# Low parts of the weights by a negated high part and an accumulating DMA, mixer passes written out, values split once

## The chip, the cores and the metric

One NeuronCore of a Trainium2 chip runs the kernel. The metric is the device time of one execution in microseconds (us). Engines are called as the profile calls them: PE (TensorE, matmul), PEld (its weight loads), DVE (VectorE), ACT (ScalarE), POOL (GpSimd), SP (SyncE, which here only issues DMAs).

## The reference

One encoder block over 512 tokens of width 1024, in fp32:

```
mod = silu(c) @ w_ada + b_ada                 # six vectors of 1024
h   = rmsnorm(x) * (1 + sc1) + sh1
B, C, u, q, k, v, gA, gB = split(h @ w_in)    # 6656 columns; 16 query heads, 4 key/value heads of 64
yA  = B * dwconv3(C * u)
yB  = windowed attention(q, k, v)             # |t-s| <= 128, q and k normed, ALiBi, a sink per head
x   = x + g1 * ((sigmoid(gA)*yA + sigmoid(gB)*yB) @ w_o)
h   = rmsnorm(x) * (1 + sc2) + sh2
a, b = split(h @ w_up)                        # 2816 columns each
x   = x + g2 * ((gelu(dwconv3(a) + bias) * b) @ w_down)
```

## The kernel before, in words

**Three products for each.** Every large product is taken in split form. A fp32 matrix is cut into a high part in the format f32r and a low part, which is the matrix minus its high part; `three` (L652 to L654) adds high·high, low·high and high·low in PSUM. So all weights must be split on the chip, and the change is about who makes their low part.

**The weight pipeline.** Weights come in 64 loads numbered n. A load is 256 columns of one weight matrix for 8 blocks of 128 rows, 1 MB in rows of 1 KB (`load`, L274, issued by SP), into slot n % 2 of `w_raw`. It has two units u of 128 columns. For each unit ACT copies `w_raw` to `w_hi` (`high`, L415), and POOL subtracts, `w_lo = w_raw - w_hi` (`low`, L341). Each step waits for the one before: `high(n)` for the load and until PE has used both units of n - 2; `low(n)` for `high(n)`; PE for the low part of its unit; `load(n + 2)` for both low parts of n, since it overwrites `w_raw`. Load 0 is the keys' weights, 1 the values', 2 to 25 the mixer's, then 4 of w_o, 22 of w_up, 12 of w_down.

**The stages.** The start normalises x, and computes the first two modulation vectors as a chain of multiply-adds on DVE (`gemv0`, L996) over 16 pieces of w_ada in a ring of 8 buffers. The keys and values are projected, the keys normed and split. The mixer is then a loop of 4 passes (`Fori`, one for each key/value head) on every engine; a pass uses 6 loads (q, C, u, B, gA, gB) and holds the attention of 4 query heads in 4 blocks of 128 queries. Then come the output projection, the second norm, the up projection (11 turns of a loop, 2 loads each) and the down projection (12 loads).

**What sets the order in a pass.** Each engine has an order written out by hand. PE has 24 slots, each with half a unit of projection (12 matmuls) and, at given slots, scores (L764), transposes of probabilities (L775) and products with values (L791). DVE starts a pass with `gemv(0)` and `gemv(1)` (L1080, L1083; eight steps a pass over `ada`, two buffers, for the other four modulation vectors), then `stage_values` (L1089, L1090; splits this head's values out of `v_nat` into `v_st`), `query_low` (L1096), query sums and norm (L1102, L954 to L962), and then for block after block `take` (L1124; scores out of PSUM), `shift` (L1131), `normalise` (L1140 to L1143), `turned_low` (L1149), `heads_out` (L1158) among the convolution's taps (L1171, L1173). ACT has the exponentials (L498), the high parts of the turned probabilities (L505), `heads_low` (L512), copies out of PSUM, and the six `high` among them. SP issues in a pass the 6 loads and, behind the loads with index 2, 3 and 4, the w_ada pieces (L318) 0 to 3, 4 and 5, 6 and 7; piece k waits until `gemv(k - 2)` has read its buffer.

Of the kernel before, what the change touches and what calls it, by code (L numbers as in the profile page):

```python
# [46 lines left out]
def encoder_block(nc, x, c, w_ada, b_ada, norm1_gain, w_in, conv_w, q_gain, k_gain, sink, w_o,  # L47
# [59 lines left out]
    with ctx:  # L107
# [41 lines left out]
        k_st = sb("k_st", [P, 2, KV, S], f32r, into=mixer)  # L149
        v_nat = sb("v_nat", [P, NB, KV * HD], into=mixer)  # L150
        q_st = sb("q_st", [P, HG, S], f32r, into=mixer)
        v_st = sb("v_st", [P, NB, 2, HD], f32r, into=mixer)
        bias = sb("bias", [P, HG, BAND], into=mixer)
# [15 lines left out]
        def hb(k):  # L169
# [19 lines left out]
        hi_ready = sem("hi_ready")  # L189
        lo_ready = sem("lo_ready")  # L190
        units_done = sem("units_done")
# [17 lines left out]
                                                   sem("pt_high"), sem("pv"))  # L209
        v_staged, shift_ready, exp_done, p_ready = sem("v_staged"), sem("shift_ready"), sem("exp_done"), sem("p_ready")  # L210
        ma_done = sem("branch_a_gated")
# [50 lines left out]
        NT = 10  # L262
        STEPS, STEPS_UP = 36, 8

# [4 lines left out]
        def _(sp):  # L269
            def load(i, per, n, src):  # L270

                if n >= 2:
                    sp.wait_ge(lo_ready, at(i, 2 * per, 2 * n - 2))
                sp.dma_start(w_raw[:, n % 2, 0:src.shape[1], :], src).then_inc(w_in_slot[n % 2], 16)  # L274
# [20 lines left out]
            for n in range(2 * KT):  # L295
# [13 lines left out]
                if n == 9:  # L309
                    sp.wait_ge(par_t, 2)  # L310
                    load(None, 0, 1, wi[:, :, COL_V:COL_V + PC])
            with sp.Fori(1, KV + 1) as g1:
                g = g1 - 1
                for n in range(NM):
                    load(g, NM, P_MIX + n, wi[:, :, bass.ds(g1 * PC + (MIX[n] - PC), PC)])
                    for k in ([], [], [0, 1, 2, 3], [4, 5], [6, 7], [])[n]:
                        sp.wait_ge(gemv_done, g * KT + (G0 + k - 1))
                        sp.dma_start(ada[:, k % 2, :],  # L318
                                     w_ada[0, k * P:(k + 1) * P, bass.ds(g1 * D + D, D)]).then_inc(ada_in[k % 2], 16)
# [14 lines left out]
        def _(pool):  # L334
            steps = Tally(pool, pool_done)

            def low(i, per, n, units=(0, 1)):

                for u in units:
                    pool.wait_ge(hi_ready, at(i, 2 * per, 2 * n + u + 1))  # L340
                    pool.tensor_tensor(w_lo[:, n % 2, u], w_raw[:, n % 2, :, u * P:(u + 1) * P],  # L341
                                       w_hi[:, n % 2, u], SUB).then_inc(lo_ready, 1)

# [13 lines left out]
            for k in range(KT):  # L357
                pool.wait_ge(xt_out, k + 1)
                pool.tensor_tensor(hT[:, k, :], xT[:, k, :], b_buf[:, 0, :], MUL).then_inc(xr_pool, 1)
            low(None, 0, 0, (0,))  # L360
            for k in range(1, HT):
                pool.wait_ge(h_h, k + 1)
                pool.wait_ge(h_f, k + 1)
                pool.tensor_tensor(h_lo[:, k, :], hb(k), h_hi[:, k, :], SUB).then_inc(h_lo_pool, 1)
            pool.wait_ge(lo_ready, 2)
            low(None, 0, 1)
# [4 lines left out]
            low(None, 0, 2)  # L371
            with pool.Fori(0, KV) as g:
                for n in range(NM):
                    if n == 5:
                        pool.wait_ge(score_free, g * (NB * HG) + (NB * HG + 2))
                    low(g, NM, P_MIX + n + 1)
                    if n == 5:

                        pool.tensor_scalar(bias[:, :, :], bias[:, :, :], 2.0 ** (-8 * HG // H), 1.0,
                                           MUL, MUL).then_inc(bias_done, 1)  # L380
# [16 lines left out]
            low(None, 0, P_UP + 1)  # L397
            with pool.Fori(0, FF // PC) as j:
                for n in range(2):
                    low(j, 2, P_UP + n + 2)  # L400
            for n in range(P_DOWN + 2, P_END):
# [4 lines left out]
        def _(act):  # L406
            steps = Tally(act, act_done)

            def high(i, per, n, units=(0, 1)):

                act.wait_ge(w_in_slot[n % 2], at(i, 16 * per // 2, 16 * (n // 2) + 16))
                if n >= 2:
                    act.wait_ge(units_done, at(i, 2 * per, 2 * n - 2))
                for u in units:
                    act.activation(w_hi[:, n % 2, u], w_raw[:, n % 2, :, u * P:(u + 1) * P],  # L415
                                   ACT.Copy).then_inc(hi_ready, 1)

            act.wait_ge(c_t, 1)
# [42 lines left out]
            act.wait_ge(units_done, 4)  # L461
            act.activation(v_nat[:, 2, :], bank[6][:, 0:PC], ACT.Copy).then_inc(o_free, 1)
            for j in range(KV):
# [5 lines left out]

            with act.Fori(0, KV) as g:  # L470
                U = 2 * P_MIX
# [177 lines left out]
        def _(pe):  # L649
# [62 lines left out]
            ada_product(PE_ADA[0])  # L712
            pe.wait_ge(lo_ready, 2)
            token_major(0, range(HT))
            pe.wait_ge(lo_ready, 4)
            pe.wait_ge(mod_read, 1)
# [13 lines left out]

            with pe.Fori(0, KV) as g:
                def unit_waits(n):
                    pe.wait_ge(lo_ready, g * (2 * NM) + (2 * P_MIX + n + 1))
                    if n in (6, 7, 8, 9):
                        pe.wait_ge(g_dve, g * 4 + (n - 5))
                    else:
                        pe.wait_ge(g_act, g * 8 + {0: 3, 1: 4, 2: 5, 3: 6, 4: 7, 5: 8, 10: 9, 11: 10}[n])
# [41 lines left out]
                def values(b, i):  # L779

                    t = TS[b][i]
                    pe.wait_ge(t_free, g * NT + (t + 3))
                    if i == 0:
                        pe.wait_ge(v_staged, g + 1)
                        pe.wait_ge(o_free, g * (2 * NB) + (2 * b + 1))
                    kb = max(b - 1, 0) + i
                    last = i == len(TS[b]) - 1
                    hi_lo = (bank[OB][:, :], v_st[:, kb], pt_hi[:, t % 2, :])
                    hi = (bank[OB][0:HD, :], v_st[:, kb, 0, :], pt_lo[:, t % 2, :])
# [52 lines left out]
            def pair(i, per, n, banks, rhs, kn=8, k_off=0, first=True, last=True, between=None):  # L842

                for u in range(2):
                    pe.wait_ge(lo_ready, at(i, 2 * per, 2 * n + u + 1))
# [8 lines left out]
            pe.wait_ge(lo_ready, 2 * P_WO + 2)  # L854
            for k in range(KT):
# [24 lines left out]
            for i, (c, f, dst) in enumerate(WO_HALVES):  # L880
                if c == 1:
                    pe.wait_ge(b_free, 2)
                pe.wait_ge(lo_ready, 2 * P_WO + f + 1)
                for k in range(KT):
# [60 lines left out]
        def _(dve):  # L945
# [86 lines left out]
            for k in range(HT):  # L1032
                modulated(k)
                if k == 0:
                    dve.wait_ge(hi_ready, 2)
                    dve.tensor_tensor(w_lo[:, 0, 1], w_raw[:, 0, :, P:2 * P], w_hi[:, 0, 1], SUB).then_inc(lo_ready, 1)
                    h_low(0)
# [15 lines left out]
            dve.wait_ge(units_done, 4)  # L1053
            for b, done in ((0, t_free), (1, t_free), (3, m_free)):
                dve.tensor_copy(v_nat[:, b, :], bank[4 + b][:, 0:PC]).then_inc(done, 1)
            for f in range(2):
# [15 lines left out]

            with dve.Fori(0, KV) as g:
                steps.enter(g, STEPS)

                def gemv(k):
# [8 lines left out]
                    ins.then_inc(gemv_done, 1)  # L1085

                def stage_values():
                    v = v_nat[:, :, bass.ds(g * HD, HD)]
                    steps.link(dve.tensor_scalar(v_st[:, :, 0, :], v, 1.0, None, MUL))  # L1089
                    dve.tensor_tensor(v_st[:, :, 1, :], v, v_st[:, :, 0, :], SUB).then_inc(v_staged, 1)  # L1090

# [327 lines left out]
```

## Time and profile before

| | |
|---|---|
| median of 3 runs | 870.67 us (870.09 to 871.1) |
| the profiled execution, first to last instruction | 870.4 us |
| mean granted clock of TensorE | 0.971 of full speed |
| PE busy | 799.9 us (92%) |
| PEld busy | 656.6 us (75%) |
| DVE busy | 615.6 us (71%) |
| POOL busy | 377.8 us (43%) |
| ACT busy | 349.3 us (40%) |
| DMA: read from HBM, mean rate | 93.43 MB, 110 GB/s |

The profiled execution's own time is its span; the median of the runs lies 0.3 us above it. Busy time is the time in which an engine had an instruction under way. An instruction's duration includes what it loses to another engine at a shared port. A fused row of the timeline ("x2") covers all the instructions in it and the short gaps between. Matmuls are pipelined: one of 512 columns is shown with about 390 ns, but in an undisturbed stretch the next one starts about 227 ns later.

### The profile page before, as it was taken

How to read it: one execution, taken by the hardware profiler on the slowest of the kernel's cores; microseconds unless marked ns; L12 is line 12 of the kernel's file. 1: busy time of each engine (PE TensorE's matmuls, PEld its weight loads, DVE VectorE, ACT ScalarE, POOL GpSimd, SP SyncE). 2: the span in 40 equal slices, each digit the busy share in tenths (PEclk: the TensorE clock that was granted, in tenths of full speed). 3: DMA queues.
4: the chain of work that ended last, by engine and by line, in shares of the span. 5: the costliest groups of instructions: out<-in, count | busy, mean ns of one | idle time of the engine just before them, and what ended most of it. 6: DMA issues, size and time to landing. Idle time of an engine off the chain costs nothing.

```text
span 870.4 us, 11305 instructions
## 1 busy us (share of the span) xinstructions
PE 799.9 (92%) x3753; PEld 656.6 (75%) x3753; DVE 615.6 (71%) x781; ACT 349.3 (40%) x589; POOL 377.8 (43%) x170
## 2 busy tenths in 40 slices
PE   3579699998999899979999899999999999999997
PEld 2468577877777777867778788888888888887886
DVE  5969899598959996898753788888888888200000
ACT  5326245454345444534542454444444443122220
POOL 3824342443325243422494434555555555445341
PEclk9679799998999999999999999999999999999999
DMA  9813612362134413541123132232222322223311
GB/s 329 303 49 131 208 57 90 117 200 69 52 140 155 134 48 99 188 146 48 48 78 116 49 98 96 96 96 96 96 96 96 96 96 84 97 85 108 120 37 48
DMA packets 79726, 95.79 MB, mean 110 GB/s; under 512 B 2210, under 2 KB 71002, under 8 KB 79706
## 3 DMA queue, kind: packets, MB, share of 16 engines
q1 hardware_dynamic: 75482, 93.43, 32.2%
q10 hardware_dynamic: 4224, 2.10, 0.8%
q8 instruction: 11, 0.18, 0.1%
q14 instruction: 9, 0.07, 0.0%
HBM read 93.43 MB, written 2.10 MB: 110 GB/s over the span
## 4 chain that ended last, share of the span: by engine, by line
PE 64%; DVE 22%; issue 9%; DMA 3%; ACT 1%; DVEq 1%; SPq 0%; ACTq 0%
PE bank L652 20%; PE bank L654 20%; PE bank L653 20%; DVE acc L1083 2%; DVE a_buf L1173 2%; DVE prob L1124 2%; DMA ada<-in_w_ada_dram 2%; DVE sm L1140 1%; DVE acc L996 1%; DVE sm L1131 1%; PE bank L791 1%; PE bank L775 1%; DVE prob L1143 1%; DVE q_st L1096 1%; DVE pt_lo L1149 1%
## 5 line engine op out<-in xcount | busy, mean ns | idle before, releaser
L341 POOL TENSOR_TENSOR w_lo<-w_raw,w_hi 128x1024 fp32r<-128x1024 f32 x127 | 333.5, 2645 | 432.7 <-ACT w_hi L415 432.7
L652 PE MATMUL bank<-h_hi,w_hi 128*128 128x512 f32 (+1 forms) x792 | 310.5, 392 | 5.5 <-DVE h_lo L1317 4.3
L653 PE MATMUL bank<-h_lo,w_hi 128*128 128x512 f32 (+1 forms) x792 | 307.0, 388 | 0.0
L654 PE MATMUL bank<-h_hi,w_lo 128*128 128x512 f32 (+1 forms) x792 | 306.7, 387 | 0.0
L652 PEld LDWEIGHTS bank<-h_hi,w_hi 128*128 128x128 f32 x792 | 151.2, 191 | 36.2 <-DVE h_lo L1317 4.0
L654 PEld LDWEIGHTS bank<-h_hi,w_lo 128*128 128x128 f32 x792 | 151.0, 191 | 30.4
L653 PEld LDWEIGHTS bank<-h_lo,w_hi 128*128 128x128 f32 x792 | 151.1, 191 | 28.5
L415 ACT ACTIVATE w_hi<-w_raw 128x1024 fp32r<-128x1024 f32 x128 | 128.7, 1051 | 108.6 <-PE bank L654 102.0
L654 PE MATMUL bank<-g_hi,w_lo 128*128 128x512 f32 x176 | 70.0, 398 | 0.0
L652 PE MATMUL bank<-g_hi,w_hi 128*128 128x512 f32 x176 | 69.9, 397 | 0.0
L653 PE MATMUL bank<-g_lo,w_hi 128*128 128x512 f32 x176 | 69.3, 394 | 0.0
L1083 DVE SCALAR_TENSOR_TENSOR acc<-ada,c_act,acc 128x1024 f32<-128x1024 f32 x28 | 61.2, 2186 | 3.1 <-DMA ada<-in_w_ada_dram 2.6
L505 ACT ACTIVATE pt_hi<-bank 128x512 fp32r<-128x512 f32 x40 | 22.2, 596 | 76.5 <-PE bank L775 76.3
L764 PE MATMUL bank<-k_st,q_st 128*128 x128 | 27.9, 337 | 21.1 <-DVE prob L1124 21.1
L1380 DVE SCALAR_TENSOR_TENSOR y_buf<-bank,mod,xT 128x512 f32<-128x512 f32 x4 | 3.0, 750 | 60.3 <-PE bank L654 60.3
L764 PEld LDWEIGHTS bank<-k_st,q_st 128*128 128x128 f32 x128 | 21.3, 196 | 28.4 <-DVE prob L1124 26.4
L1380 DVE SCALAR_TENSOR_TENSOR a_buf<-bank,mod,xT 128x512 f32<-128x512 f32 x4 | 3.0, 752 | 54.9 <-PE bank L654 54.9
L1372 DVE TENSOR_TENSOR g_lo<-y_buf,g_hi 128x512 f32 x22 | 39.7, 1803 | 2.7
L607 ACT ACTIVATE pad_f<-bank 128x512 f32<-128x512 f32 x22 | 13.1, 599 | 70.7 <-PE bank L654 70.7
L1354 DVE SCALAR_TENSOR_TENSOR a_buf<-pad_f,par,a_buf 128x512 f32<-128x512 f32 x22 | 37.6, 1708 | 3.3 <-DVE a_buf L1352 1.7
L653 PEld LDWEIGHTS bank<-g_lo,w_hi 128*128 128x128 f32 x176 | 33.1, 188 | 8.1
L654 PEld LDWEIGHTS bank<-g_hi,w_lo 128*128 128x128 f32 x176 | 33.0, 188 | 7.8
(175 smaller groups left out, 1076.5 us busy)
## 6 DMA issues: line engine op xcount, KB each, us to landing
w_raw<-in_w_in_dram SPq DMA_DIRECT2D x26, 1024.0 KB, 5.1
ada<-in_w_ada_dram SPq DMA_DIRECT2D x48, 512.0 KB, 6.0
w_raw<-in_w_up_dram SPq DMA_DIRECT2D x22, 1024.0 KB, 5.1
w_raw<-in_w_down_dram SPq DMA_DIRECT2D x8, 1024.0 KB, 4.9
w_raw<-in_w_o_dram SPq DMA_DIRECT2D x4, 1024.0 KB, 5.0
w_raw<-in_w_down_dram SPq DMA_DIRECT2D x4, 768.0 KB, 4.2
x_nat<-in_x_dram SPq DMA_DIRECT2D x4, 512.0 KB, 4.9
out_dram<-b_buf ACTq DMA_DIRECT2D x4, 256.0 KB, 2.3
```

What stands on the lines that cost most here:

```text
L341: pool.tensor_tensor(w_lo[:, n % 2, u], w_raw[:, n % 2, :, u * P:(u + 1) * P], w_hi[:, n % 2, u], SUB).then_inc(lo_ready, 1)
L415: act.activation(w_hi[:, n % 2, u], w_raw[:, n % 2, :, u * P:(u + 1) * P], ACT.Copy).then_inc(hi_ready, 1)
L505: act.activation(pt_hi[:, t % 2, :], bank[TB[t % 2]][:, :], ACT.Copy).then_inc(pt_h, 1)
L652: pe.matmul(dst, w_h, rhs_hi, start=first, stop=False)
L653: pe.matmul(dst, w_h, rhs_lo, start=False, stop=False)
L654: return pe.matmul(dst, w_l, rhs_hi, start=False, stop=last)
L764: mm = pe.matmul(dst, q_st[:, h, b * P:(b + 1) * P], k_st[:, p, bass.ds(g, 1), j0:j1].rearrange("p a n -> p (a n)"), start=(p == 0), stop= ...
L1083: ins = dve.scalar_tensor_tensor(acc[:, :], ada[:, k % 2, :], c_act[:, 0, k:k + 1], acc[:, :], MUL, ADD)
L1124: dve.scalar_tensor_tensor(prob[:, b % 2, h, 0:w], bank[SC[h % 2]][:, 0:w], sm[:, 6, b, h:h + 1], bias[:, h, c0:c0 + w], MUL, ADD).then_in ...
L1173: steps.link(dve.scalar_tensor_tensor(a_buf[:, u, :], pad[u][:, tap:tap + S], w(tap), a_buf[:, u, :], MUL, ADD))
L1354: dve.scalar_tensor_tensor(a_buf[:, u, :], pad[u][:, 2:S + 2], w(PA_FW + 2 * FT), a_buf[:, u, :], MUL, ADD).then_inc(conv_done, 1)
L1372: dve.tensor_tensor(lo, y_buf[:, u, :], hi, SUB).then_inc(ffn_tiles, 1)
```

## The change

- **Low parts.** ACT writes the high part as before, and then a second copy of the same weights with a scale of -1.0 into `w_lo`, which is rounded to the same value with its sign turned. POOL then issues a DMA that adds `w_raw` to `w_lo` in place. There is a semaphore for each slot and unit (`lo_in`), counted up by 16 by each DMA. PE and SP wait on these. In the first load DVE used to make the low part of unit 1 (L1036); POOL's DMA now makes it too.
- **Values.** The 4 blocks of projected values are split into `v_st` for all 4 heads once, straight from PSUM (ACT the high part, DVE the low part), in place of a copy to `v_nat` (L462, L1055) and a split in each pass (`stage_values`).
- **Loops.** The 4 mixer passes are written out on all five engines, as is POOL's part of the up projection.

```diff
-        v_nat = sb("v_nat", [P, NB, KV * HD], into=mixer)
-        v_st = sb("v_st", [P, NB, 2, HD], f32r, into=mixer)
+        v_st = sb("v_st", [P, NB, KV, 2, HD], f32r, into=mixer)
...
+        V_ORDER = (2, 3, 0, 1)
+        def v_heads(b):
+            return bank[4 + b][:, 0:PC].rearrange("p (j d) -> p j d", d=HD)
+        def wait_low(eng, i, per, n, u):
+            eng.wait_ge(lo_in[n % 2][u], at(i, 8 * per, 16 * (n // 2) + 16))
...
             def load(i, per, n, src):
                 if n >= 2:
-                    sp.wait_ge(lo_ready, at(i, 2 * per, 2 * n - 2))
+                    for u in range(2):
+                        wait_low(sp, i, per, n - 2, u)
...
-            with sp.Fori(1, KV + 1) as g1:
-                g = g1 - 1
+            for g in range(KV):
+                g1 = g + 1
...
                 for u in units:
                     pool.wait_ge(hi_ready, at(i, 2 * per, 2 * n + u + 1))
-                    pool.tensor_tensor(w_lo[:, n % 2, u], w_raw[:, n % 2, :, u * P:(u + 1) * P],
-                                       w_hi[:, n % 2, u], SUB).then_inc(lo_ready, 1)
+                    pool.wait_ge(neg_ready, at(i, 2 * per, 2 * n + u + 1))
+                    pool.dma_start(w_lo[:, n % 2, u], w_raw[:, n % 2, :, u * P:(u + 1) * P],
+                                   accum_op=ADD).then_inc(lo_in[n % 2][u], 16)
...
                 for u in units:
                     act.activation(w_hi[:, n % 2, u], w_raw[:, n % 2, :, u * P:(u + 1) * P],
                                    ACT.Copy).then_inc(hi_ready, 1)
+                    act.activation(w_lo[:, n % 2, u], w_raw[:, n % 2, :, u * P:(u + 1) * P],
+                                   ACT.Copy, scale=-1.0).then_inc(neg_ready, 1)
...
-            act.activation(v_nat[:, 2, :], bank[6][:, 0:PC], ACT.Copy).then_inc(o_free, 1)
+            for b in V_ORDER:
+                act.activation(v_st[:, b, :, 0, :], v_heads(b), ACT.Copy).then_inc(v_high, 1)
...
                 def unit_waits(n):
-                    pe.wait_ge(lo_ready, g * (2 * NM) + (2 * P_MIX + n + 1))
+                    wait_low(pe, g, NM, P_MIX + n // 2, n % 2)
...
-                        pe.wait_ge(v_staged, g + 1)
...
-                if k == 0:
-                    dve.wait_ge(hi_ready, 2)
-                    dve.tensor_tensor(w_lo[:, 0, 1], w_raw[:, 0, :, P:2 * P], w_hi[:, 0, 1], SUB).then_inc(lo_ready, 1)
...
-            for b, done in ((0, t_free), (1, t_free), (3, m_free)):
-                dve.tensor_copy(v_nat[:, b, :], bank[4 + b][:, 0:PC]).then_inc(done, 1)
+            for n, b in enumerate(V_ORDER):
+                dve.wait_ge(v_high, n + 1)
+                dve.tensor_tensor(v_st[:, b, :, 1, :], v_heads(b), v_st[:, b, :, 0, :],
+                                  SUB).then_inc((t_free, t_free, o_free, m_free)[b], 1)
...
-                def stage_values():
-                    v = v_nat[:, :, bass.ds(g * HD, HD)]
-                    steps.link(dve.tensor_scalar(v_st[:, :, 0, :], v, 1.0, None, MUL))
-                    dve.tensor_tensor(v_st[:, :, 1, :], v, v_st[:, :, 0, :], SUB).then_inc(v_staged, 1)
```

## Rows read from the trace of the kernel before

**Rows 1.** Busy time by stage (columns: busy us of each engine, clock, DMA share, GB/s).
```profile
80.00:171.00 91.00, 81.43 (x378) 65.54 (x377) 76.75 (x116) 42.75 (x86) 33.17 (x13) 0.94 0.35 116
735.00:866.00 131.00, 129.17 (x568) 103.55 (x566) 15.19 (x17) 26.75 (x31) 52.95 (x22) 1.00 0.27 85
```
**Rows 2.** PE's timeline in the second mixer pass: where it sat idle before an instruction.
```profile
190.29 0.90 PE L764 MATMUL bank<-k_st,q_st 128*128 x4 [1.52 <-DVE prob L1124]
202.96 1.65 PE L764 MATMUL bank<-k_st,q_st 128*128 x4 [2.84 <-DVE prob L1124]
221.99 1.09 PE L775 MATMUL bank<-ident,prob 128*128 128x128 f32 x8 [1.34 <-DVE prob L1143]
223.41 1.14 PE L764 MATMUL bank<-k_st,q_st 128*128 x4 [0.33 <-DVE prob L1124]
```
**Rows 3.** PE's timeline in the first mixer pass, its longest idle time.
```profile
100.79 1.22 PE L764 MATMUL bank<-k_st,q_st 128*128 x4 [6.68 <-DVE prob L1124]
```
**Rows 4.** Busy time and granted clock around that wait in passes one and two.
```profile
95.00:110.00 15.00, 9.21 (x31) 7.62 (x32) 12.41 (x22) 3.25 (x5) 1.43 (x1) 0.66 0.59 194
200.00:210.00 10.00, 7.16 (x24) 5.96 (x24) 8.72 (x16) 0.10 (x1) 1.29 (x1) 0.66 0.32 105
```
**Rows 5.** DVE's timeline in the second pass.
```profile
172.38 2.48 DVE L1089 TENSOR_SCALAR v_st<-v_nat 128x256 fp32r x1
174.90 0.43 DVE L1090 TENSOR_TENSOR v_st<-v_nat,v_st 128x256 fp32r<-128x256 f32 x1
...
196.00 6.38 DVE L1083 SCALAR_TENSOR_TENSOR acc<-ada,c_act,acc 128x1024 f32<-128x1024 f32 x2 [0.38 <-DMA ada<-in_w_ada_dram]
...
215.34 2.66 DVE L1173 SCALAR_TENSOR_TENSOR a_buf<-pad_f,par,a_buf 128x512 f32<-128x512 f32 x1 [0.15 <-DVE a_buf L1173]
218.12 2.15 DVE L1140 TENSOR_TENSOR sm<-sm 128x4 f32<-128x4 f32 x1
...
229.65 0.48 DVE L1171 TENSOR_SCALAR a_buf<-pad_f,par 128x512 f32<-128x512 f32 x1
```
**Rows 6.** POOL's timeline in the second pass.
```profile
195.60 5.70 POOL L341 TENSOR_TENSOR w_lo<-w_raw,w_hi 128x1024 fp32r<-128x1024 f32 x2 [7.27 <-ACT w_hi L415]
214.49 5.77 POOL L341 TENSOR_TENSOR w_lo<-w_raw,w_hi 128x1024 fp32r<-128x1024 f32 x2 [13.19 <-ACT w_hi L415]
```
**Rows 7.** All instructions of lines L1083, L415 and L341 (ns min/median/max).
```profile
L1083 DVE SCALAR_TENSOR_TENSOR acc<-ada,c_act,acc x28: 1273/1286/3317, 81.7 to 381.3; 128x1024 f32<-128x1024 f32 x28
L415 ACT ACTIVATE w_hi<-w_raw x128: 1040/1049/1083, 23.9 to 846.3; 128x1024 fp32r<-128x1024 f32 x128
L341 POOL TENSOR_TENSOR w_lo<-w_raw,w_hi x127: 2343/2463/3388, 30.6 to 848.8; 128x1024 fp32r<-128x1024 f32 x127
```
**Rows 8.** ACT's timeline in the second pass.
```profile
181.61 2.01 ACT L415 ACTIVATE w_hi<-w_raw 128x1024 fp32r<-128x1024 f32 x2
188.40 0.22 ACT L435 ACTIVATE st<-st 128x16 f32<-128x16 f32 x1 [2.23 <-DVE st L954]
251.04 1.09 ACT L505 ACTIVATE pt_hi<-bank 128x512 fp32r<-128x512 f32 x2 [0.36 <-PE bank L775]
```
**Rows 9.** SP's timeline in the second pass: DMAs issued.
```profile
188.50 0.38 SPq L274 DMA_DIRECT2D w_raw<-in_w_in_dram  x1
191.99 2.31 SPq L318 DMA_DIRECT2D ada<-in_w_ada_dram  x2
```
**Rows 10.** Two loads of the up projection (columns as in rows 1).
```profile
562.40:584.20 21.80, 21.80 (x98) 18.06 (x97) 18.71 (x17) 8.77 (x11) 10.88 (x4) 1.00 0.30 95
```
**Rows 11.** DMA: queue of the stores (packets, MB, share of 16 engines); issue to landing.
```profile
q10 hardware_dynamic: 4224, 2.10, 0.8%
...
w_raw<-in_w_up_dram SPq DMA_DIRECT2D x22, 1024.0 KB, 5.1
```
**Rows 12.** The start: DVE's timeline, and one stretch (columns as in rows 1).
```profile
39.06 12.83 DVE L996 SCALAR_TENSOR_TENSOR acc<-ada,c_act,acc 128x1024 f32<-128x1024 f32 x6
...
30.00:40.00 10.00, 6.63 (x31) 5.04 (x31) 9.79 (x11) 4.83 (x6) 7.06 (x5) 0.76 1.00 355
```
**Rows 13.** DVE near the second norm.
```profile
499.99 2.18 DVE L1317 SCALAR_TENSOR_TENSOR h_lo<-a_buf,mod,h_hi 128x256 fp32r<-128x256 f32 x1
```

More of the change, by code:

```diff
@@ L189, in encoder_block @@
         hi_ready = sem("hi_ready")
-        lo_ready = sem("lo_ready")
+        neg_ready = sem("minus_high_ready")
+        lo_in = [[sem(f"low_added{s}{u}") for u in range(2)] for s in range(2)]
         units_done = sem("units_done")
@@ L209, in encoder_block @@
                                                    sem("pt_high"), sem("pv"))
-        v_staged, shift_ready, exp_done, p_ready = sem("v_staged"), sem("shift_ready"), sem("exp_done"), sem("p_ready")
+        v_high, shift_ready, exp_done, p_ready = sem("v_high"), sem("shift_ready"), sem("exp_done"), sem("p_ready")
         ma_done = sem("branch_a_gated")
@@ L262, in encoder_block @@
         NT = 10
-        STEPS, STEPS_UP = 36, 8
+        STEPS_UP = 8
         block = ctx.enter_context(nc.Block())
@@ L359, in _ @@
                 pool.tensor_tensor(hT[:, k, :], xT[:, k, :], b_buf[:, 0, :], MUL).then_inc(xr_pool, 1)
-            low(None, 0, 0, (0,))
+            low(None, 0, 0)
             for k in range(1, HT):
@@ L364, in _ @@
                 pool.tensor_tensor(h_lo[:, k, :], hb(k), h_hi[:, k, :], SUB).then_inc(h_lo_pool, 1)
-            pool.wait_ge(lo_ready, 2)
             low(None, 0, 1)
@@ L371, in _ @@
             low(None, 0, 2)
-            with pool.Fori(0, KV) as g:
+            for g in range(KV):
                 for n in range(NM):
@@ L397, in _ @@
             low(None, 0, P_UP + 1)
-            with pool.Fori(0, FF // PC) as j:
-                for n in range(2):
-                    low(j, 2, P_UP + n + 2)
+            for n in range(P_UP + 2, P_DOWN + 2):
+                low(None, 0, n)
             for n in range(P_DOWN + 2, P_END):
@@ L468, in _ @@
                                    ACT.Copy).then_inc(kh_done, 1)
-            with act.Fori(0, KV) as g:
+            for g in range(KV):
                 U = 2 * P_MIX
@@ L712, in _ @@
             ada_product(PE_ADA[0])
-            pe.wait_ge(lo_ready, 2)
+            wait_low(pe, None, 0, 0, 0)
+            wait_low(pe, None, 0, 0, 1)
             token_major(0, range(HT))
-            pe.wait_ge(lo_ready, 4)
+            wait_low(pe, None, 0, 1, 0)
+            wait_low(pe, None, 0, 1, 1)
             pe.wait_ge(mod_read, 1)
@@ L729, in _ @@
                 mm.then_inc(kt_done, 1)
-            with pe.Fori(0, KV) as g:
+            for g in range(KV):
                 def unit_waits(n):
-                    pe.wait_ge(lo_ready, g * (2 * NM) + (2 * P_MIX + n + 1))
+                    wait_low(pe, g, NM, P_MIX + n // 2, n % 2)
                     if n in (6, 7, 8, 9):
@@ L787, in values @@
                     last = i == len(TS[b]) - 1
-                    hi_lo = (bank[OB][:, :], v_st[:, kb], pt_hi[:, t % 2, :])
-                    hi = (bank[OB][0:HD, :], v_st[:, kb, 0, :], pt_lo[:, t % 2, :])
+                    hi_lo = (bank[OB][:, :], v_st[:, kb, g], pt_hi[:, t % 2, :])
+                    hi = (bank[OB][0:HD, :], v_st[:, kb, g, 0, :], pt_lo[:, t % 2, :])
                     for n, args in enumerate((hi, hi_lo) if last else (hi_lo, hi)):
@@ L844, in pair @@
                 for u in range(2):
-                    pe.wait_ge(lo_ready, at(i, 2 * per, 2 * n + u + 1))
+                    wait_low(pe, i, per, n, u)
                     for k in range(kn):
@@ L853, in _ @@
             pe.wait_ge(score_free, 2 + KV * NB * HG)
-            pe.wait_ge(lo_ready, 2 * P_WO + 2)
+            wait_low(pe, None, 0, P_WO, 0)
+            wait_low(pe, None, 0, P_WO, 1)
             for k in range(KT):
@@ L882, in _ @@
                     pe.wait_ge(b_free, 2)
-                pe.wait_ge(lo_ready, 2 * P_WO + f + 1)
+                wait_low(pe, None, 0, P_WO + f // 2, f % 2)
                 for k in range(KT):
@@ L893, in _ @@
             pe.wait_ge(a_free, 2)
-            pe.wait_ge(lo_ready, 2 * P_UP + 2)
+            wait_low(pe, None, 0, P_UP, 0)
+            wait_low(pe, None, 0, P_UP, 1)
             for c in range(2):
@@ L1071, in _ @@
             dve.wait_ge(sink_in, 16)
-            with dve.Fori(0, KV) as g:
-                steps.enter(g, STEPS)
+            for g in range(KV):
                 def gemv(k):
@@ L1196, in _ @@
                 gemv(1)
-                stage_values()
                 query_low(0)
@@ L1250, in _ @@
                 merge(1)
-                steps.leave(KV)
             steps.link(dve.scalar_tensor_tensor(amp[:, 1, :], mod[:, 4 * KT:5 * KT], 1.0, par[:, PA_G2:PA_G2 + KT],
```

## The prediction

> **What bounds the kernel now.** I read busy time by stage first. In the up and down projections PE is never idle: 21.80 of 21.80 us at full clock [rows 10], 129.17 of 131 at the end [rows 1]. Nothing that frees another engine can shorten these some 360 us; the change can only lose there. Such a stretch of 21.8 us holds two loads, so one load is used up in 10.9 us, the rate that the low parts must keep. In the mixer PE is busy for 81.43 of 91 us and DVE for 76.75 [rows 1]. PE's timeline says what ends the gaps: it waits for DVE four times in the second pass, 1.52 + 2.84 + 1.34 + 0.33 = 6.0 us [rows 2]. The third and fourth passes repeat this to 0.1 us. The first pass has 6.68 us at one place [rows 3], some 9.3 in all. So at most 9.3 + 3 × 6.0 = 27 us of waits can go, and what the clock gives back: around the longest wait it falls to a mean of 0.66 in the first two passes [rows 4], that is to 1.2 GHz in part, after PE had been idle.
>
> Why is DVE late? Two of its steps of L1083, each 1.27 us alone, took 6.38 us [rows 5], beside POOL's two subtractions at 195.60 [rows 6]. The pair at 214.49 lies over a tap of 2.66 and a 4-element addition of 2.15 us that moves next to nothing [rows 5]. L1083 has a shortest time of 1.273 and a longest of 3.317 us [rows 7]: 2.0 us is what a collision costs DVE. There are 12 subtractions in a pass, so at most 24 us are lost; since not each of them meets a DVE instruction, I estimate 18.
>
> **The change part by part.**
>
> *POOL's subtraction goes.* 127 × 2.46 us leave POOL [rows 7]. DVE gets up to 18 us a pass back, but only what ends a PE wait counts.
>
> *Values.* DVE loses 2.48 + 0.43 us a pass [rows 5], of which 2 us is again the collision. The single split costs DVE four subtractions of that kind (0.43) chained behind ACT copies, in place of three copies: 0.8 us later at the keys, just before the first pass.
>
> *ACT's negated copy.* 128 more of 1.05 us [rows 7], so each `high` with two units grows from 2.0 to 4.2 us. In the up and down projections ACT is busy for 8.8 of 21.8 us [rows 10] and has room. In a pass it is in order with the attention. The `high` at 181.61 stands before the squares of the second query unit: they move from 183.5 to 185.6, the query norm's root, 188.40 before [rows 8], to about 187.4 (0.9 us of copy and squares behind, DVE's sums and variance 0.9, now without stall). So of DVE's gain of some 5 us up to there only 1 to 1.2 remain. The last `high` of a pass stands before `heads_low(2)` and the high parts at 251.04 [rows 8]; ACT comes 1.9 us later there, of which I estimate that PE, which used the result about a microsecond after it was ready, feels 0.8: a new wait.
>
> *The accumulating DMA.* No row of this trace shows one, so I bound it. A unit is 1024 rows of 512 bytes, 64 for each of the 16 DMA engines. Stores in packets of that size take 0.008 × 16 × 870.4 / 4224 = 26 ns each [rows 11]: 64 × 26 ns = 1.7 us for a unit, the lower end. A load of 1024 packets of 1 KB takes 0.30 × 16 × 10.9 / 1024 = 51 ns for each [rows 10], 3.3 us of all engines. An accumulating packet reads 512 bytes from `w_raw` and 512 from `w_lo`, the reading of one such packet: I take 51 ns, 3.3 us a unit. If reading twice and writing once each cost a packet of their own it is 3 × 26 = 79 ns, 5.1 us a unit, the upper end. From issue to landing a load takes 5.1 us [rows 11], 1.8 beyond its packets; with the same on top a unit lands in 5.1, say 5.3 us with POOL's own issue. That issue is bounded by SP's (0.38 us, rows 9) and by the POOL instruction it replaces (2.46 us, rows 7); up to there it hides in POOL's idle time.
>
> *Does it keep up?* Per load: 2 × 3.3 + 3.3 = 9.9 of 10.9 us of DMA, 91%. The limit is (10.9 - 3.3) / 2 = 3.8 us a unit, or 60 ns a packet. In time: slots come free at T, PE wants unit 0 at T + 10.9. High part and negated part take 2.1 us, a copy before them 0.6, which leaves 8.2 us for a landing that I put at 5.3. Cost in the projections: nothing, covered by this margin of 2.9 us.
>
> *SP's queue.* A load now waits for the landing, not for POOL, and the w_ada pieces are queued behind it. In the second pass the load was issued at 188.50 and piece 6 at 191.99 [rows 9], and `gemv(6)` waited for it until 196.00 [rows 5]. New: negated parts done at 185.8, landed at 191.1, load, then piece 6 behind it: 191.1 + 3.3 + 1.6 (half a load) + 1.8 = 197.9. `gemv(6)` and `gemv(7)` then take 2.6 in place of 6.4 us, and PE's wait at 202.96 ends at 201.1: 1.9 us earlier, not 5. This is the total gained up to that point of a pass, the 1.2 included. Then 1.34 + 0.33 = 1.6 us of waits at 222 to 223 [rows 2] go, since the stalls of rows 5 before them go. Less 0.8 at the end: 2.7 us a pass.
>
> *Sum for the mixer:* 3 × 2.7 = 8; first pass 5, as 4 of its 6.68 us are stalls beside subtractions; clock 3, of the 2 to 3 us that each of the two stretches of rows 4 loses. Together 16 us.
>
> *The start.* Six steps of L996 took 12.83 us [rows 12], with POOL's subtractions of load 1 beside them; unstalled, at the shortest of L1083 for the same form, they take 7.8. But the DMA engines are full until about 42 us (share 1.00, rows 12), and two units add up to 6.5 us to the stream that feeds these steps. I take 1.5 us of the 5. The keys' norm gains 1.3, values take 0.8 back. Together 2 us.
>
> *The second norm.* Its stalled rows, as the one of 2.18 us in place of 0.47 [rows 13], come to 3 us; ACT's two extra copies there take 2.1 back: 1 us.
>
> *Loops written out.* No wait in the rows lies at a pass's border, so nothing; the end to be feared, instructions that come late, shows nowhere in the stretches that are straight code already.
>
> Sum: 870.4 - 16 - 2 - 1 = 851.4 us for the profiled execution, which lay 0.3 us below the median: 851.7.
>
> **Rivals.**
>
> *Slower: the accumulating DMAs don't keep up.* Place: the up and down projections, 33 loads of 10.9 us. It decides from 3.8 us a unit. At the upper end of 5.1 a load takes 2 × 5.1 + 3.3 = 13.5 us, 2.6 more: 33 × 2.6 = 86 us, less the gains elsewhere, about 935. POOL making 1024 rows' descriptors slower than 5.4 us a unit would do the same. For it: 91% is close, and nothing shows the price of the adding. Against: the nearest row gives 51 ns, and DMA has a share of 0.30 there now. 28%, half of it below 935.
>
> *No gain: late landings.* If a unit lands in 7.8 us, the load in the sum above goes out at 193.6, piece 6 lands at 200.4, and PE's wait ends at about 204.1, 1.1 us later than now. Less 1.6, plus 0.8: 0.3 us a pass, all gains of the mixer gone, about 869 with the start's (862 to 880). What could delay by 2.5 us is a turned collision: POOL's issue held by DVE, as DVE is held now. The Trainium skill, "SBUF — State Buffer", section "Who interferes with whom", says that DVE's two-port forms (fp32 copies and tensor_scalar from SBUF to SBUF) keep POOL from writing a DMA's descriptors, and gives 620 ns growing to 3100; by that rule, 2.5 us more, the result would be this rival's. No row here shows a DMA issued by POOL, so the trace doesn't settle it; against it, DVE's instructions of that kind are short (0.48 us, rows 5), so one of them alone holds POOL for less. 16%.
>
> *More gain.* If a unit lands in under 4 us, most of the 27 us of waits and the clock go: 825 to 835. 6%.
>
> **How the numbers follow.** The forecast, 835 to 862, has 50%. A measurement of this kernel can tell about 0.2%, 1.7 us. Faster: 50 + 6 + 5 of the late landings = 61%; within: 5 of these and 1 = 6%; slower: 28 + 5 = 33%. The range reaches from 832 to 935, the upper end of the DMA's price; beyond lie 14% above, some 3% below. The likeliest case alone is 835 to 862.
>
> **What would show it.** Right: DVE's L1083 all near 1.29 us, DVE busy in the mixer down by some 60 us, PE's wait before the 3rd score group shorter but still there and ended by DVE behind a w_ada piece; PE without idle time from 505 on; DMA share there near 0.9. Wrong: PE waiting on a DMA into `w_lo` in the projections, a load used up in over 10.9 us, or SP's loads issued over 8 us after ACT's negated part.

## The result and the profile after

The changed kernel takes 958.3 us in the median (956.0 to 963.3), beside 870.9 us for the kernel before: a ratio of 1.100, 95% interval 1.098 to 1.102. The forecast was 851.7 us, the range ended at 935. The page of the kernel after, with busy time of each engine, the DMA queues (packets, MB, share of 16 engines), the groups of the new DMA and the new copies, and the issues:

```profile
span 957.6 us, 10582 instructions
...
PE 816.2 (85%) x3753; PEld 667.0 (70%) x3753; DVE 442.3 (46%) x773; ACT 463.4 (48%) x715; POOL 243.6 (25%) x171
...
q0 software_dynamic: 133120, 67.12, 62.6%
q1 hardware_dynamic: 75482, 93.43, 29.5%
...
L353 POOL DMA_DIRECT2D w_lo<-w_raw x128 | 199.0, 1564 | 641.4 <-ACT w_lo L427 616.8
L427 ACT ACTIVATE w_lo<-w_raw 128x1024 fp32r<-128x1024 f32 x128 | 133.6, 1044 | 0.0
...
w_lo<-w_raw POOLq DMA_DIRECT2D x128, 512.0 KB, 8.7
...
ada<-in_w_ada_dram SPq DMA_DIRECT2D x48, 512.0 KB, 9.4
```

DVE did get its time back: 615.6 us busy before, 442.3 now. What is new is queue q0 with 62.6% of all DMA engines' time. 0.626 × 16 × 957.6 us over 133,120 packets is 72 ns a packet, or 4.7 us of all engines for a unit (1040 packets). With the other queues the DMA engines are 93% busy over the whole span. (A landing time is the time from the issue of a DMA until its data is there.)

Where the 87 us went, by landmarks in both traces (first mixer step of DVE in each pass; first and last `pad_f` copy of the up projection; last product of the down projection):

| stretch | before | after | more |
|---|---|---|---|
| start, to the first pass | 80.9 | 84.3 | 3.4 |
| first three passes | 271.7 | 302.3 | 30.7 |
| fourth pass, output projection, second norm | 156.2 | 165.3 | 9.1 |
| up projection | 218.0 | 240.4 | 22.4 |
| up to the first output of down | 37.7 | 41.8 | 4.1 |
| down projection | 101.1 | 118.6 | 17.5 |

**The up projection** in a window of the kernel after (columns as in rows 1):

```profile
600.00:700.00 100.00, 93.90 (x404) 76.25 (x403) 42.93 (x67) 52.48 (x64) 24.79 (x16) 0.98 1.04 176
```

PE is busy for 93.9 of 100 us, where it had no idle time [rows 10], and the DMA share is 1.04, where it was 0.30: full. Two turns of the loop, read off the first `pad_f` copy of each (594.17 and 690.12, four turns apart), take 24.0 us a turn, 12.0 a load, against 10.9. A share above 1 means that the recorded times of packets overlap a little.

**The mixer.** A pass takes 100.8 us in the mean of the first three, 90.6 before. PE's waits there (us in total, times, longest), first in the kernel before, then in the kernel after:

```profile
PE bank L764 <- DVE prob L1124: 21.1, 11, 6.7
...
PE bank L779 <- DVE prob L1134: 55.9, 8, 13.2
PE bank L665 <- DMA w_lo<-w_raw: 7.0, 4, 3.7
```

PE hardly waits for low parts in a pass; it waits for DVE's takes of scores, 55.9 us against 21.1. And DVE, though idle half of the time, is late because of this, in the second pass:

```profile
203.82 1.28 DVE L1098 SCALAR_TENSOR_TENSOR acc<-ada,c_act,acc 128x1024 f32<-128x1024 f32 x1 [6.56 <-DMA ada<-in_w_ada_dram]
...
218.85 1.28 DVE L1098 SCALAR_TENSOR_TENSOR acc<-ada,c_act,acc 128x1024 f32<-128x1024 f32 x1 [10.04 <-DMA ada<-in_w_ada_dram]
```

These are `gemv(4)` and `gemv(6)`; `gemv(7)` follows at 220.58. The chain of work that ended last, in the stretch before `gemv(7)`, shows the whole path, and SP's timeline the issues between (0.38 us a load, 3.49 for two pieces):

```profile
191.23 15.61 DMA w_lo<-w_raw
...
208.87 11.69 DMA ada<-in_w_ada_dram
```
```profile
206.91 0.38 SPq L285 DMA_DIRECT2D w_raw<-in_w_in_dram  x1
207.34 3.49 SPq L329 DMA_DIRECT2D ada<-in_w_ada_dram  x2
```

The unit issued at 191.23 lands 15.6 us later, while its neighbour unit, a load and two w_ada pieces are on the same DMA engines. Only then does SP issue the next load, and behind it the pieces 6 and 7. Piece 7, sharing the engines with the next two units, lands 11.7 us later. In the kernel before the load went out at 188.50 and `gemv(6)` started at 196.00 [rows 5, 9]: 18.1 and 25.6 us after the first step of that pass (170.39), against 26.2 and 38.2 us here (180.70).

### The profile page after: what moved, and what is told of

It is laid out like the page before. It is cut to its first block, busy times and chain, and to the rows that moved or that the text cites. A ratio compares the mean times of both kernels' runs of the same rounds, so it can differ in the third digit from the quotient of the medians.

```text
span 957.6 us, 10582 instructions
## 1 busy us (share of the span) xinstructions
PE 816.2 (85%) x3753; PEld 667.0 (70%) x3753; DVE 442.3 (46%) x773; ACT 463.4 (48%) x715; POOL 243.6 (25%) x171
## 3 DMA queue, kind: packets, MB, share of 16 engines
q0 software_dynamic: 133120, 67.12, 62.6%
q1 hardware_dynamic: 75482, 93.43, 29.5%
## 4 chain that ended last, share of the span: by engine, by line
PE 42%; DMA 40%; POOL 5%; ACT 5%; issue 4%; DVE 2%; SPq 1%; ACTq 0%; POOLq 0%; DVEq 0%
DMA w_lo<-w_raw 23%; PE bank L665 12%; PE bank L666 12%; PE bank L667 12%; DMA w_raw<-in_w_up_dram 7%; DMA ada<-in_w_ada_dram 6%; DMA w_raw<-in_w_down_dram 3%; ACT w_lo L427 2%; POOL w_lo L353 2%; PE bank L805 2%; PE bank L790 2%; PE bank L779 2%; POOL hT L371 2%; ACT w_hi L425 1%; DVE acc L1098 1%
## 5 line engine op out<-in xcount | busy, mean ns | idle before, releaser
L353 POOL DMA_DIRECT2D w_lo<-w_raw x128 | 199.0, 1564 | 641.4 <-ACT w_lo L427 616.8
L665 PE MATMUL bank<-h_hi,w_hi 128*128 128x512 f32 (+1 forms) x792 | 315.8, 399 | 27.6 <-DMA w_lo<-w_raw 23.1
L425 ACT ACTIVATE w_hi<-w_raw 128x1024 fp32r<-128x1024 f32 x128 | 134.5, 1050 | 140.4 <-PE bank L667 68.1
L666 PEld LDWEIGHTS bank<-h_lo,w_hi 128*128 128x128 f32 x792 | 153.1, 193 | 28.6
L427 ACT ACTIVATE w_lo<-w_raw 128x1024 fp32r<-128x1024 f32 x128 | 133.6, 1044 | 0.0
L665 PE MATMUL bank<-g_hi,w_hi 128*128 128x512 f32 x176 | 73.0, 415 | 14.3 <-DMA w_lo<-w_raw 14.3
L779 PE MATMUL bank<-k_st,q_st 128*128 128x256 f32 (+1 forms) x128 | 29.3, 356 | 55.9 <-DVE prob L1134 55.9
L1098 DVE SCALAR_TENSOR_TENSOR acc<-ada,c_act,acc 128x1024 f32<-128x1024 f32 x28 | 35.9, 1283 | 78.4 <-DMA ada<-in_w_ada_dram 78.2
L665 PEld LDWEIGHTS bank<-g_hi,w_hi 128*128 128x128 f32 x176 | 34.4, 196 | 24.6 <-DMA w_lo<-w_raw 12.9
L1359 DVE TENSOR_SCALAR a_buf<-pad_f,par 128x512 f32<-128x512 f32 x22 | 12.0, 547 | 83.2 <-ACT pad_f L620 83.2
L511 ACT ACTIVATE prob<-prob,sm 128x256 f32<-128x256 f32 (+1 forms) x64 | 35.2, 558 | 5.9 <-DVE sm L1144 5.9
```

Source lines behind the costliest of these rows:

```text
L353: pool.dma_start(w_lo[:, n % 2, u], w_raw[:, n % 2, :, u * P:(u + 1) * P], accum_op=ADD).then_inc(lo_in[n % 2][u], 16)
L427: act.activation(w_lo[:, n % 2, u], w_raw[:, n % 2, :, u * P:(u + 1) * P], ACT.Copy, scale=-1.0).then_inc(neg_ready, 1)
L511: act.activation(prob[:, b % 2, h, 0:w], prob[:, b % 2, h, 0:w], ACT.Exp, bias=sm[:, 1, b, h:h + 1], accum_out=sm[:, 3, b, h:h + 1]).then_ ...
L665: pe.matmul(dst, w_h, rhs_hi, start=first, stop=False)
L666: pe.matmul(dst, w_h, rhs_lo, start=False, stop=False)
L779: mm = pe.matmul(dst, q_st[:, h, b * P:(b + 1) * P], k_st[:, p, bass.ds(g, 1), j0:j1].rearrange("p a n -> p (a n)"), start=(p == 0), stop= ...
```

## The experiments

Each edit is against the changed kernel unless it says otherwise. "Pass" is the mean of the first three mixer passes, "up" the up projection between its landmarks; both are read from the profiled execution. Passes are counted from DVE's first step, so a first pass whose first step was late looks shorter.

| run | time us | ratio to before (95%) | pass | up |
|---|---|---|---|---|
| before | 870.9 | | 90.6 | 218.0 |
| changed | 958.3 | 1.100 (1.098 to 1.102) | 100.8 | 240.4 |
| e1_pool_low | 874.0 | 1.001 (0.998 to 1.004) | 89.5 | 217.9 |
| e3_neg_copy_pool_add | 874.7 | 1.003 (1.001 to 1.004) | 90.0 | 218.0 |
| e5_plain_copy_dma | 872.3 | 1.000 (0.999 to 1.002) | 91.0 | 217.9 |
| e6_rows_of_4k | 895.9 | 1.026 (1.021 to 1.031) | 96.8 | 218.0 |
| f1_fewer_w_ada | 902.5 | 1.035 (1.031 to 1.039) | 87.2 | 237.9 |
| f4_rows_4k_fewer_w_ada | 844.8 | 0.969 (0.967 to 0.970) | 85.1 | 217.9 |
| g1_before_fewer_w_ada | 871.6 | 1.000 (0.998 to 1.001) | 90.0 | 218.0 |
| e7_half_by_dma | 886.8 | 1.017 (1.016 to 1.019) | 92.1 | 217.9 |
| f2_rows_4k_late_gemv | 863.5 | 0.991 (0.989 to 0.992) | 90.2 | 217.9 |
| c1_before_late_gemv | 881.1 | 1.011 (1.009 to 1.012) | 93.1 | 218.0 |
| c2_rows_4k_late_gemv_first3 | 867.9 | 0.997 (0.995 to 0.998) | 90.8 | 218.0 |
| c3_after_late_gemv | 919.2 | 1.056 (1.054 to 1.058) | 92.3 | 237.3 |

**1. The parts of the change without the DMA.**

```diff
-                    pool.dma_start(w_lo[:, n % 2, u], w_raw[...], accum_op=ADD).then_inc(lo_in[n % 2][u], 16)
+                    pool.tensor_tensor(w_lo[:, n % 2, u], w_raw[...], w_hi[:, n % 2, u], SUB).then_inc(...)
...
-                    act.activation(w_lo[:, n % 2, u], w_raw[...], ACT.Copy, scale=-1.0).then_inc(neg_ready, 1)
```

> The changed kernel with POOL's subtraction back in place of ACT's negated copy and the accumulating DMA; written-out passes and the single split of the values stay. Theory A (the DMA engines are full: 64 accumulating packets of 73 ns per engine and unit, 4.7 us): all of the loss is in the low parts, so this runs at 862 to 871 us, a few us under the kernel before for the DVE work of 2.9 us a pass that is gone. Rival C (written-out passes make instructions late): over 880 us, with idle time of every engine at the borders of the passes.

Measured: 874.0 us, no difference from the kernel before, but 3 us over the window expected. That the loss is in the low parts stands, C falls: written-out loops cost nothing that can be told. But the few microseconds expected of the values did not come either (the 89.5 us a pass come from a first step at 85.5 us in place of 80.9; the second and third passes take 182.4 us together, 182.2 before). In all four passes the collision with POOL now falls on the first step, which took 0.75 us and takes 2.7 to 2.9:

```profile
L1092 DVE TENSOR_SCALAR acc<-ada,c_act x4: 2694/2882/2882, 85.5 to 354.0; 128x1024 f32<-128x1024 f32 x4
```

**2. ACT's extra copy, with the adding done by a POOL instruction.**

```diff
-                    pool.dma_start(w_lo[:, n % 2, u], w_raw[...], accum_op=ADD)
+                    pool.tensor_tensor(w_lo[:, n % 2, u], w_raw[...], w_lo[:, n % 2, u], ADD)
```

> The changed kernel with ACT's negated copy kept, but POOL adding w_raw to w_lo with an instruction in place of the DMA. Theory A: ACT's 128 extra copies of 1.05 us hide; at most 8 us above the first run of this call. Rival B (ACT's copies delay the attention's chain and the second norm): 20 us or more above it, with PE waiting for ACT's lines in the mixer.

Measured: 874.7 us, 0.6 us over the run without ACT's copies. ACT is busy for 463.2 us, 120 more, and they hide. Rival B falls. The 0.6 us is a net figure: DVE's busy time fell by 45 us in the same run, so a cost of the copies can be covered by that gain.

**3. The DMA without its adding.**

```diff
-                    pool.dma_start(w_lo[:, n % 2, u], w_raw[...], accum_op=ADD)
+                    pool.dma_start(w_lo[:, n % 2, u], w_raw[...])
```

> The changed kernel with POOL's DMA as a plain copy of w_raw into w_lo: it leaves the adding out (the low parts are then the whole weights). Same number of DMAs, rows and waits. Theory A, if the price of a packet is that of reading twice: packets of some 26 to 40 ns, DMA share under 0.8 in the up projection, 840 to 865 us. If the price lies in what POOL's kind of DMA costs whatever it does (small rows, descriptors from its rings): packets stay near 73 ns and the time within 3% of the changed kernel's 958 us.

Its queue, POOL's issue and its DMA, and then a window of the up projection (columns as in rows 1):

```profile
q0 software_dynamic: 133120, 67.12, 45.5%
...
L353 POOL DMA_DIRECT2D w_lo<-w_raw x128 | 113.0, 883 | 648.2 <-ACT w_lo L426 648.1
...
w_lo<-w_raw POOLq DMA_DIRECT2D x128, 512.0 KB, 3.9
```
```profile
600.00:700.00 100.00, 100.00 (x443) 82.84 (x442) 47.01 (x74) 58.12 (x71) 16.65 (x19) 1.00 0.85 194
```

0.455 × 16 × 870.1 / 133,120 is 48 ns a packet, 3.1 us a unit: the adding costs 24 ns a packet. POOL's issue takes 0.88 us in place of 1.56, so the adding, not the number of rows alone, made it long. At 2 × 3.1 + 3.3 = 9.5 us a load, under 10.9, PE never idles in the up projection. So the number of DMAs and their waits are not the trouble there. Packets, share and time missed the expectation: 48 ns for 26 to 40, 0.85 for under 0.8, and 872 us for 840 to 865. In the mixer DVE still waited 41 us for w_ada pieces (2.6 us in the kernel before), and PE 22.7 us for takes.

**4. The same adding in rows of 4 KB.** `w_raw` is laid out by units, so a unit is 128 rows of 4 KB on both sides. A load becomes two DMAs of 512-byte rows.

```diff
-        w_raw = sb("w_raw", [P, 2, 8, PC])
+        w_raw = sb("w_raw", [P, 2, 2, 8, P])
...
-                sp.dma_start(w_raw[:, n % 2, 0:src.shape[1], :], src).then_inc(w_in_slot[n % 2], 16)
+                for u in range(2):
+                    sp.dma_start(w_raw[:, n % 2, u, 0:src.shape[1], :],
+                                 src[:, :, u * P:(u + 1) * P]).then_inc(w_in_slot[n % 2], 16)
```

> The changed kernel with w_raw laid out by units, so that the accumulating DMA moves rows of 4 KB in place of 512 bytes; a load becomes two DMAs whose rows are 512 bytes in place of 1 KB. Theory A with a price per packet: the unit falls from 4.7 to 2.5 to 3.3 us of all engines, the DMA share of the up projection under 0.9, 845 to 880 us. If the adding has a price per byte (512 KB in 4.7 us): no better than 940 us.

The queue, the DMA, and POOL's issue in a later run of the same layout:

```profile
q0 software_dynamic: 18432, 67.12, 39.7%
...
w_lo<-w_raw POOLq DMA_DIRECT2D x128, 512.0 KB, 5.5
```
```profile
L355 POOL DMA_DIRECT2D w_lo<-w_raw x128: 852/862/1167, 30.8 to 842.5; - x128
```

0.397 × 16 × 892.6 / 128 / 16 is 2.8 us a unit in place of 4.7, with every byte still added; the issue takes 0.86 us in place of 1.56. So most of the expected price per packet is there, but not all goes by the row: with an eighth of the rows a unit still costs 59% of the time. An estimate from these two runs, if both parts add: 34 ns a row and 2.5 us for the 512 KB. The loads, now in rows of 512 bytes, pay for it: q1 takes 318 us of all engines (0.356 × 892.6), 280 before. The up projection is back at 218.0 us with a DMA share of 0.86. The time is above the expected 845 to 880 us: what is left of the loss lies in the mixer, 96.8 us a pass, with 37.0 us of PE's waits for takes.

**5. The mixer's loss: late w_ada pieces.** The pieces 2 to 7 of each pass are not loaded, in the changed kernel, in the one with rows of 4 KB, and, as control, in the kernel before.

```diff
-                    for k in ([], [], [0, 1, 2, 3], [4, 5], [6, 7], [])[n]:
+                    for k in ([], [], [0, 1], [], [], [])[n]:
...
-                    dve.wait_ge(ada_in[k % 2], g * (8 * KT) + (16 * (k // 2) + 16))
+                    dve.wait_ge(ada_in[k % 2], g * 16 + 16)
```

> The changed kernel without the loads of w_ada's pieces 2 to 7 in the mixer (24 of 32 pieces; the steps of L1098 then work on the pieces 0 and 1, so four of the six modulation vectors are wrong). Theory A2 (the mixer's loss is w_ada pieces that come late behind a load which waits for an accumulating DMA): a pass falls from 100.8 us to 90 or less, the whole to 905 to 920 us; the up projection keeps its 240 us. Rival (the mixer loses by PE waiting on w_lo or on ACT): passes stay over 95 us.

> The layout with rows of 4 KB and the same w_ada pieces left out. Shows what DVE freed of POOL's subtractions is worth with both limits away: theory A2: passes of 82 to 88 us, the whole 840 to 862 us. If it stays at 870 or more, the freed DVE was worth nothing and my forecast's gain was wrong for another reason than late pieces.

> The kernel before without the w_ada pieces 2 to 7 in the mixer (four of the six modulation vectors are wrong): the counterpart of the run with rows of 4 KB and fewer pieces, 844.8 us. If the 27 us between that run and the kernel before are mostly DVE freed of POOL's subtractions (theory A3), the kernel before gains little from the missing pieces, since DVE waited 2.6 us for them in all: 862 to 871 us. If they are mostly the missing pieces: 845 to 855 us.

In the changed kernel the pass falls from 100.8 to 87.2 us, while the up projection keeps 237.9: two separate losses. (The whole, 902.5 us, lies 2.5 us under the window expected.) PE's longest waits in the mixer, first in the control, then with rows of 4 KB:

```profile
PE bank L764 <- DVE prob L1124: 21.1, 11, 6.6
```
```profile
PE bank L792 <- DVE prob L1155: 5.4, 3, 2.6
```

The control gains nothing from the missing pieces: 871.6 us, its PE waits 21.1 us for takes as ever. The other runs at 844.8, 26 to 27 us faster. So DVE freed of POOL's subtractions is worth 27 us in this kernel, net of what ACT's copies and the DMA cost, but only if the pieces come in time.

**6. Half and half.** Unit 0 by the DMA, unit 1 by POOL's subtraction; ACT makes the negated copy of unit 0 alone.

```diff
+                    if u == 0:
                         pool.dma_start(w_lo[:, n % 2, u], w_raw[...], accum_op=ADD).then_inc(lo_in[n % 2][u], 16)
+                    else:
+                        pool.tensor_tensor(w_lo[:, n % 2, u], w_raw[...], w_hi[:, n % 2, u], SUB).then_inc(...)
```

> The changed kernel with unit 0 by ACT's negated copy and the DMA, unit 1 by POOL's subtraction as before (SP's loops of the up and down projections are written out too). Theory A: per load 4.7 + 3.3 = 8.0 us of DMA are under the 10.9 us that PE needs, so the up projection is back at 218 us with PE never idle; the whole 865 to 885 us, the rest in the mixer. If POOL's kind of DMA stops something else than the DMA engines, the up projection keeps some half of its 22 us loss.

Again 72 ns a packet, and the up projection at 217.9 us with a DMA share of 0.72: under the limit nothing is lost there. So the time on the DMA engines is the trouble in the projections. The whole is 2 us above the expected window. PE waited 7.63 us for `w_lo` in the start, where the first units meet the w_ada stream, and 5.80 in the first pass.

**7. A version that beats both.** Rows of 4 KB, and in each pass `gemv(4)` behind the first shift, `gemv(5)` behind the second, `gemv(6)` and `gemv(7)` in the third block, so that no take stands behind a piece that may be late.

```diff
                 take(0, (0, 1))
-                gemv(4)
                 take(0, (2, 3))
-                gemv(5)
                 shift(0)
-                gemv(6)
-                gemv(7)
+                gemv(4)
                 take(1, (0, 1))
...
                 shift(1)
+                gemv(5)
...
                 take(2, (0, 1))
+                gemv(6)
...
                 shift(2)
+                gemv(7)
...
-                    if slot in (13, 17):
-                        ada_turn((slot - 13) // 4)
+                    if slot in (15, 19):
+                        ada_turn((slot - 15) // 4)
```

> The layout with rows of 4 KB, and DVE's steps 4 to 7 of the other modulation vectors moved later in each pass (4 behind the first shift, 5 behind the second, 6 and 7 in the third block; PE's turns of them two slots later), so that no take of scores stands behind a late w_ada piece. Everything is computed. Theory A2: PE's wait for the takes falls from 37 us to under 20, the whole 855 to 872 us. If another wait takes its place: 880 to 892 us.

863.5 us, 0.9% under the kernel before (interval 0.8 to 1.1%), in the window expected. Hardly anything of it shows in the first three passes (90.2 us against 90.6): the up projection starts 8.3 us earlier, and 7.4 of them come after the first step of the fourth pass. PE waited 1.5 us for takes in all. Its waits in the mixer, the longest two groups (L816 are its turns of the modulation sums):

```profile
PE bank L816 <- DVE acc L1100: 7.2, 4, 1.9
PE bank L807 <- DVE pt_lo L1161: 6.6, 4, 2.0
```

**8. Controls of that version.** The same order in the kernel before, the same order with rows of 512 bytes, and the version with the first three loads' low parts left to POOL.

> The kernel before with nothing but the later order of DVE's steps 4 to 7 and of PE's turns of them (POOL's subtractions stay). If the gain of the late order with rows of 4 KB came from the order alone: 860 to 865 us here too. Theory A3 (late pieces and POOL's collisions each hold DVE, and only both removed free PE): 866 to 872 us.

> The changed kernel (rows of 512 bytes) with the late order alone. Theory A2: the mixer's passes fall from 100.8 to some 92 to 95 us, the up and down projections keep their loss of 40 us: 915 to 935 us.

> Rows of 4 KB and the late order, and the low parts of loads 0 to 2 by POOL's subtraction, so that in the start no accumulating DMA meets the stream of w_ada, whose DMA engines are full. PE's wait for w_lo falls from 9.5 us at 43 us back to some 4; the whole 855 to 863 us. If the start isn't on the path that sets the end: within 2 us of 863.5.

The order alone makes the kernel before slower, 881 us, more than either theory said: DVE still collides with POOL, and PE now also waits 8.8 us in all for the late steps. With rows of 512 bytes the order takes the pass from 100.8 to 92.3 us, and the projections keep their loss. So the gain needs all three: DVE free of POOL, the cheaper DMA in rows of 4 KB, and the pieces off the path of the takes. The last control is a miss. With POOL's subtractions back in the start, PE's wait of 9.5 us for `w_lo` shrinks to 2.9, but six steps of `gemv0` take their 12.84 us again [rows 12], and the whole is 4 us slower:

```profile
40.26 12.84 DVE L1023 SCALAR_TENSOR_TENSOR acc<-ada,c_act,acc 128x1024 f32<-128x1024 f32 x6
```

PE's wait was not on the path that sets the end of the start; the modulation's chain was: the first low part behind it starts 1.8 us later than in the version above, and so does the first step of the mixer. Where the other 2.5 us were lost was not traced.

## Why the prediction was wrong

The step that failed is the price of the accumulating DMA, and behind it the conclusion "Does it keep up?". I took 51 ns a packet and 3.3 us a unit; it is 72 ns and 4.7 us. I had set 60 ns and 3.8 us as the limit, with 79 ns as the upper end, so the rival of DMAs that don't keep up was the case, and I gave it 28%. Its arithmetic held for its place, nearly: 2 × 4.7 + 3.3 = 12.7 us a load, measured 12.0. By that rival's sum 4.7 us a unit would give 851.7 + 33 × 1.8, some 911 us; the projections lost less than it says (40 us in place of 59), and the other 47 of the 87 us were lost where the rival still counted my gains. The nearest row was a load's packet of 1 KB, on the ground that both read 1 KB. A plain copy in the same rows, 48 ns, shows the wrong ground: POOL's packets of 512 bytes between `w_raw` and `w_lo` already cost nearly twice a store's 26 ns [rows 11], before any adding.

The second step that failed is the landing in "SP's queue": 5.3 us for a unit, then 3.3 + 1.6 + 1.8 us for the load and the piece, each as if nothing else were on the engines (together 197.8, not 197.9; nothing hangs on that). The 5.1 us behind it is a median of loads in the up projection, where the DMA share is 0.30. In the stretch of the sum it was 0.80 already in the kernel before, and the change adds two units there. The window before, and then the plain copies of experiment 3, whose unit lands in 3.9 us in the median but in 9.4 in this place:

```profile
181.50:196.00 14.50, 12.97 (x62) 10.52 (x61) 13.09 (x20) 5.42 (x9) 5.98 (x3) 1.00 0.80 259
```
```profile
DMA to landing us min/median/max: 3.8/3.9/11.6
...
182.29 9.36 DMA w_lo<-w_raw
```

So even a cheap packet did not bring the gain. With rows of 4 KB, 5.5 us to the landing in the median, close to my 5.3, a pass takes 96.8 us, 6.2 more than before, where I had forecast 2.7 less; and in experiment 3 the condition of my rival "More gain" (a unit lands in under 4 us) was met and the time was 872, not 825 to 835. The mixer's w_ada pieces land in 6.9 and 6.8 us there, 4.5 in the kernel before, 7.2 in the changed one (medians).

I also let the two bad rivals exclude each other. The "late landings" rival named SP's queue as its place, load behind landing, w_ada piece behind load, and put the landing at 7.8 us. In the changed kernel the median is 8.7 us and the worst 15.6: dear packets made the landings later still. The passes lost 31 us in three and part of 9 in the fourth, in place of my gain of 16; the rival's result, 869 us, was far too mild, and the range ended 23 us short.

What held:

- *DVE gets its time back.* All 28 steps of L1098 take 1.27 to 1.29 us, as said; the longest was 3.3 [rows 7]. DVE's 27 us of worth, once everything else was cleared away, is as large as the 27 us of waits that I counted as the most that can go. That is partly chance: between control and run PE's waits in the mixer fell by 17 us (28.6 to 11.7). The rest, the clock among it (0.977 and 0.983), I did not separate.
- *Up and down projections can only lose.* They did: 22 + 18 us.
- *ACT's copies hide*, to 0.6 us net; *written-out loops cost nothing* that can be told.

What did not hold beside the price and the landing: the start lost 3.4 us for my 2 us gained, and not as I feared. The units did not hold up the stream of w_ada: the six steps of `gemv0` take 8.24 us in place of 12.83, near the 7.8 of the sum. But PE waited 11.77 us for the low parts of load 0, where its longest wait for a low part was 4.04 us before, and the first step of the mixer waited 2.46 us for its piece. I had put PE's wait at nothing.

```profile
38.86 8.24 DVE L1012 SCALAR_TENSOR_TENSOR acc<-ada,c_act,acc 128x1024 f32<-128x1024 f32 x6
```
```profile
43.75 0.55 PE L665 MATMUL bank<-w_hi,h_hi 128*128 128x256 f32 x1 [11.77 <-DMA w_lo<-w_raw]
```

And the values' split was worth nothing with POOL's subtractions in place, because a collision only moved to the next DVE instruction.

On the rule of the Trainium skill, "SBUF — State Buffer", section "Who interferes with whom", that DVE can keep POOL from writing descriptors: POOL's issue took 1.54 us at the least and 1.55 in the median, so it was mostly undisturbed, and with rows of 4 KB 0.85 and 0.86. So far as the length of the issue shows it, this was not what made landings late. The figures of 620 and 3100 ns stand in the Trainium skill, "SBUF — State Buffer", in another section, "A bandwidth-pool intuition that's wrong (but worth ruling out)"; no run here shows them.

## What to carry to other kernels

Before handing work to the DMA engines, add up their time in the tightest steady stretch, by rows as well as by bytes; an accumulating DMA cost 72 ns for a row of 512 bytes here, and in rows of 4 KB 2.8 us for 512 KB over 16 engines. Do the same for the busiest burst, not only for the mean: a landing time read where the engines are 30% busy did not hold where they were 80% busy. When a queue waits for a transfer where it waited for an instruction, everything behind it in that queue inherits the landing time under load; look for who consumes that, here DVE's in-order stream in front of PE. And a freed engine shows its worth only when the next wait is moved out of its way too: here one edit cost 87 us, while with two more the kernel came out 8 us under the one before.

## What the runs showed that I had not expected

- A 512 KB unit costs 4.7 us of all DMA engines in rows of 512 bytes and 2.8 us in rows of 4 KB, with the same bytes read, added and written; POOL's issue falls from 1.56 to 0.86 us. A plain copy in the same rows of 512 bytes is issued in 0.88 us, so it is rows and adding together that made it long.
- POOL's adding of `w_raw` to `w_lo` in place disturbs DVE less than the subtraction of `w_hi` did: DVE busy 569.9 us against 614.6, with about the same POOL time (374.5 and 375.7). I did not look into why.
- The loads' own packets hardly suffered: the share of q1 is 29.5% of 957.6 us, 60 ns a packet, 59 before. Their landings in the mixer did not change either (5.1 us, 5.0 before), but the w_ada pieces behind them land in 7.2 us in place of 4.5. So it is more work on the engines, not a slower packet of the loads, that made the pieces late.
